# One product of 512 columns instead of two of 256 in the query, gate and output projections of the first block

## The chip, the cores and the metric
The kernel runs on one core of a Trainium2 chip. The metric is the device time of one execution in microseconds (us), the median of several runs. A profile of one execution comes beside it. Engines: PE (TensorE) multiplies, PEld is its weight load, DVE (VectorE), ACT (ScalarE) and POOL (GpSimd) do the rest, and SP issues most DMAs.

## The reference
Two transformer blocks run over 256 tokens in float32. Only the first block's mixer matters here (16 learned tokens are put in front, so 272):

```
u = rms_norm(h, mix_pre_g);  proj = u @ w_in
hq, hf, hi, hg, cq, ckv, kpe, gates = split(proj)
y_a = hgrn2_mixer(hq, hf, hi, hg, ...) @ w_hg_o     # qh = silu(hq): a scan over the tokens
y_b = mla_mixer(cq, ckv, kpe, ...)     @ w_mla_o    # attention with latent q, k, v
gate_a, gate_b = split(sigmoid(gates + b_gate))
mixed = (gate_a * y_a + gate_b * y_b) @ w_out
h = h + rms_norm(mixed, mix_post_g)                 # then the feed-forward part, then block 2
```

## The kernel before, in words
Each float32 matrix is used as a high part (rounded to what a fast product takes) and a low part (the rest). A product is high weights by high tokens, high weights by low tokens, and low weights by high tokens, added in PSUM.

**Weights.** They come in slabs of 16 blocks of 128 x 128 (SP's queue, three buffers `raw`), and a slab is two *units* of eight blocks. A step `split u` makes the parts of unit u: `wh` by ACT or DVE (a copy with rounding), `wl` by POOL or DVE (a subtraction). The letters in `MADE` (L412) say who does which; they are not changed. A unit can be split when its place in `WH` and `WL` was read by PE.

**Tokens.** `OPERAND[src][:, k, part, :]` holds token rows k, both parts side by side: x1 is the normed input (272 columns a part), oh the scan's output, om the attention's (256 a part).

**Tiles.** `gemm name n` computes 128 output columns of a projection for all tokens: eight row blocks (k), three products of 256 columns each (`three`, L861) into the first 256 columns of a PSUM bank. `evac name n` takes the result from PSUM. Names: `hq` (query of the scan, 8 tiles), `gate` (16 tiles, 0 to 7 for y_a, 8 to 15 for y_b), `ya` and `yb` (the two output projections, 8 each), `kn`, `qn`, `qpe`, `ckv`, `cq`, `kpe`, `hf`, `hg` and others, which stay as they are. The feed-forward tiles g1, u1, g2, u2 are already `FOLDED` (L842, L961): one product of 512 columns (high weights by both parts) and one of 256 (low weights), after which the two halves of the bank are added.

**Order.** One list `ORDER` of steps is written by `segments` and woven by the strings in `MIX`. Each engine walks that list and issues its own instructions of each step, so every engine has a fixed order; semaphores tie them. The stages here, with the time of the trace: hq tiles (69 to 92 us), then the scan (to 185) with its steps `level` (PE), `decay` (DVE, multiplies queries and keys), `k_turn`, `state`, `read` and the latent norms `lat` between tiles hg, ckv, kpe, cq and gate 0 to 7; then kn, qn, qpe (to 211); gate 8 to 15 and ya between the attention's heads (`m_score`, `m_exp`, `m_turn`, `m_value`, to 282); yb (to 305); `down out1` 0 to 3 and the first `tail` (w_out, whose weights are units 76 to 83).

**Before the change.** In `scalar` and `vector`: hq n is a sigmoid on ACT from PSUM and a multiplication on DVE with PSUM (L1317, L1646). gate n is one tanh on ACT from PSUM (L1326). ya n is one DVE product with PSUM (L1667). yb n is a DVE product with PSUM, a DVE addition of ya's part, an ACT copy that makes the high part of `mx` and a DVE product minus that for the low part (L1340, L1672); `mx` is what `down out1` multiplies. gate and ya use PSUM banks 0, 1, 2 in turn, yb 0 to 3, hq all eight; a bank is free when the last reader of a tile is done.

Of the kernel before, what the change touches and what calls it, by code (L numbers as in the profile page):

```python
# [556 lines left out]
def rf(ap):  # L557
    return ap.bitcast(FP)


def program(nc, dr):
    ctx = ExitStack()
    with ctx:
# [278 lines left out]
        FOLDED = ("g1", "u1", "g2", "u2")  # L842
# [11 lines left out]
        def tensor(e):  # L854
# [43 lines left out]
            for step in ORDER:  # L898
# [52 lines left out]
                elif kind == "gemm":  # L951
# [4 lines left out]
                    for k in range(k0, k1):  # L956
                        u, o = divmod(BLOCK_AT[step] + k - k0, 8)
                        unit(u, o)
                        e.wait_ge(*act.at(part(src, "h", k)))
                        e.wait_ge(*dve.at(part(src, "l", k)))  # L960
                        if name in FOLDED:  # L961
                            e.matmul(b.rearrange("p (a t) -> p a t", a=2), whi(u, o), OPERAND[src][:, k, :, :], start=k == 0, stop=False)
                            m = e.matmul(b[:, 0:256], wlo(u, o), operand(src, k, 0), start=False, stop=k == 7)
                        else:
                            m = three(b[:, 0:t.stop - t.start], whi(u, o), wlo(u, o), operand(src, k, 0)[:, t],
                                      operand(src, k, 1)[:, t], k == 0, k == kt - 1)
                        names = ([("used", u)] if o == 7 else []) + ([use] if k == kt - 1 else [])
                        if names:
                            m.then_inc(*pe.up(*names))
# [296 lines left out]
        def scalar(e):  # L1266
            e.dma_start(cst[:, 0:128], dr["cst"][:, 0:128]).then_inc(*in_id.up("all", by=16))
            e.wait_ge(*dve.at("one"))
            e.activation(stat("one"), stat("one"), ACT.Sqrt)
            for step in ORDER:  # L1270
# [37 lines left out]
                elif kind == "evac":  # L1308
# [8 lines left out]
                    elif name in ("hq", "hg"):  # L1317
# [8 lines left out]
                    elif name == "gate":  # L1326
                        e.wait_ge(*pe.at(use))
                        e.wait_ge(*dve.at("half_bias"))
                        if n >= 8:
                            e.wait_ge(*pe.at(("read", 1, 1)))  # L1330
                        e.activation((GA0 if n < 8 else GA1)[:, n % 8, :], b[:, 0:256], ACT.Tanh, bias=sc("b_gate", n),
                                     scale=0.5).then_inc(*act.up(step))
                        banks.ended(use, act.now())
                    elif name in ("kn", "qn"):
                        e.wait_ge(*pe.at(use))
# [227 lines left out]
        def vector(e):  # L1563
            e.memset(rf(R2[:, 0:512]), 1.0).then_inc(*dve.up("unread"))
            for name in ("one", ("one", "out1"), ("one", "ffn1"), ("one", "out2"), ("one", "ffn2")):
                e.memset(stat(name), 1.0).then_inc(*dve.up(name))
            for step in ORDER:
# [62 lines left out]
                elif kind == "evac":  # L1630
# [15 lines left out]
                    elif name in ("hq", "hg"):  # L1646
                        v = (Qr if name == "hq" else SG)[:, n, :]
# [19 lines left out]
                    elif name == "ya":  # L1667
                        e.wait_ge(*act.at(("evac", "gate", n)))
                        e.wait_ge(*pe.at(use))
                        e.scalar_tensor_tensor(GA0[:, n, :], GA0[:, n, :], 1.0, b[:, 0:256], ALU.add, ALU.mult).then_inc(*dve.up(step))  # L1670
                        banks.ended(use, dve.now())
                    elif name == "yb":  # L1672
                        g = GA1[:, n, :]
                        e.wait_ge(*act.at(("evac", "gate", 8 + n)))
                        e.wait_ge(*pe.at(use))
                        e.scalar_tensor_tensor(g, g, 1.0, b[:, 0:256], ALU.add, ALU.mult).then_inc(*dve.up(step))
                        banks.ended(use, dve.now())
# [641 lines left out]
```

## Time and profile before

| | us |
|---|---|
| median of 3 runs (lowest, highest) | 927.81 (926.04, 928.13) |
| profiled execution, its own time | 925.93 |
| its span, first to last instruction | 924.1 |
| PE busy in the span | 902.4 |
| DVE, ACT, POOL busy | 678.8, 465.2, 223.1 |

The span is what the engines' rows cover; the rest of the execution's time lies around it. The granted TensorE clock was 0.997 of full speed. Matmul rows overlap, so the pace of PE is read from start to start. In a timeline a row is a start, a duration, the engine, the line, the operation, what it writes and reads by the program's names, and how many instructions it merges; a bracket gives the engine's idle time before it and who ended it. All helpers record at one line per kind, so groups are told apart by names and shapes: `pb` is PSUM, `R` the token operands, `wh` and `wl` the weight parts, `FA` the working area, `st` small statistics.

### The profile page before, as it was taken

The numbers are of one execution on the slowest core, as the hardware profiler recorded it, in microseconds if no ns is written. First come the engines' busy times: TensorE is split into PE (matmuls) and PEld (weight loads), VectorE is DVE, ScalarE is ACT, GpSimd is POOL, SyncE is SP. The second block draws the span as 40 slices with busy tenths as digits, with TensorE's granted clock in tenths as the row PEclk, the third lists the DMA queues.
The fourth block names the chain that finished last, engine by engine and source line by source line (L and its number), as shares of the span: only waits on it lengthen the run. The fifth ranks groups of instructions, "written<-read, shape, count | busy, mean of one in ns | idle before, by whom it ended". The sixth has DMA issues, their size and how long they took to land.

```text
span 924.1 us, 16815 instructions
## 1 busy us (share of the span) xinstructions
PE 902.4 (98%) x6767; PEld 800.5 (87%) x6767; DVE 678.8 (73%) x1274; ACT 465.2 (50%) x936; POOL 223.1 (24%) x120
## 2 busy tenths in 40 slices
PE   9999999999999999999999999999999999999996
PEld 8879999889999888888888799887988888888885
DVE  5924986658655888767576768868888888788885
ACT  6334336564443574434444647776634445544343
POOL 3433421441213211642314342231100211210121
PEclk9999999999999999999999999999999999999999
DMA  8454444233433645655545354324445555455521
GB/s 296 150 205 143 176 141 139 84 122 138 137 105 130 227 175 207 226 184 194 197 162 222 136 191 157 106 87 163 179 157 208 183 188 209 155 223 183 214 105 46
DMA packets 23181, 153.67 MB, mean 166 GB/s; under 512 B 2864, under 2 KB 3248, under 8 KB 5568
## 3 DMA queue, kind: packets, MB, share of 16 engines
q1 hardware_dynamic: 22384, 150.43, 45.6%
q0 software_dynamic: 576, 2.10, 0.6%
q8 instruction: 54, 0.88, 0.4%
q14 instruction: 23, 0.19, 0.1%
q10 hardware_dynamic: 144, 0.07, 0.0%
HBM read 151.28 MB, written 1.05 MB: 165 GB/s over the span
## 4 chain that ended last, share of the span: by engine, by line
PE 60%; DVE 26%; ACT 10%; issue 4%; DVEq 0%; ACTq 0%
PE pb L506 58%; DVE wl L515 11%; ACT wh L512 4%; DVE FA L515 4%; DVE FA L518 4%; DVE FA L521 3%; ACT FA L512 3%; PE pb L509 2%; DVE wh L530 1%; ACT R L512 1%; DVE X L521 1%; DVE R L521 1%; DVE st L518 0%; DVE post L518 0%; DVE FA L524 0%
## 5 line engine op out<-in xcount | busy, mean ns | idle before, releaser
L506 PE MATMUL pb<-R,wh 128*128 128x256 f32 (+2 forms) x2224 | 550.4, 326 | 5.9 <-ACT R L512 2.0
L506 PE MATMUL pb<-R,wl 128*128 128x256 f32 (+1 forms) x1512 | 422.7, 281 | 0.0
L506 PEld LDWEIGHTS pb<-R,wh 128*128 128x128 f32 x2224 | 372.2, 189 | 45.4 <-ACT R L512 3.5
L515 POOL TENSOR_TENSOR wl<-raw,wh 128x1024 fp32r<-128x1024 f32 (+1 forms) x80 | 195.7, 2450 | 632.8 <-ACT wh L512 522.7
L515 DVE TENSOR_TENSOR wl<-raw,wh 128x1024 fp32r<-128x1024 f32 (+1 forms) x198 | 262.0, 1345 | 82.1 <-ACT wh L512 80.5
L506 PEld LDWEIGHTS pb<-R,wl 128*128 128x128 f32 x1512 | 284.3, 188 | 2.0 <-issue 0.3
L512 ACT ACTIVATE wh<-raw 128x1024 fp32r<-128x1024 f32 (+1 forms) x219 | 222.8, 1044 | 52.8 <-PE pb L506 50.8
L506 PE MATMUL pb<-wh,R 128*128 128x512 f32 (+2 forms) x724 | 234.4, 388 | 4.1 <-DVE R L515 2.1
L506 PEld LDWEIGHTS pb<-wh,R 128*128 128x128 f32 (+1 forms) x724 | 134.4, 186 | 36.7 <-ACT R L512 4.0
L512 ACT ACTIVATE FA<-pb 128x256 f32<-128x256 f32 (+7 forms) x240 | 94.0, 414 | 125.9 <-PE pb L506 111.0
L506 PE MATMUL pb<-wl,R 128*128 128x512 f32 (+2 forms) x372 | 143.3, 385 | 0.0
L512 ACT ACTIVATE FA<-FA 128x256 f32<-128x256 f32 (+4 forms) x69 | 28.0, 405 | 141.3 <-DVE FA L521 121.8
L506 PEld LDWEIGHTS pb<-wl,R 128*128 128x128 f32 (+1 forms) x372 | 68.2, 183 | 12.7 <-issue 0.2
L515 DVE TENSOR_TENSOR FA<-pb,FA 128x256 f32<-128x256 f32 (+1 forms) x128 | 53.9, 426 | 34.3 <-ACT FA L512 34.3
L515 DVE TENSOR_TENSOR FA<-FA 128x256 f32<-128x256 f32 (+7 forms) x120 | 68.9, 598 | 8.5 <-ACT FA L512 3.3
L506 PE MATMUL pb<-FA 128*32 128x16 f32 (+6 forms) x1456 | 60.9, 216 | 0.2
L512 ACT ACTIVATE R<-FA 128x256 fp32r<-128x256 f32 (+1 forms) x66 | 28.4, 431 | 61.7 <-DVE FA L515 61.7
L506 PEld LDWEIGHTS pb<-FA 128*32 128x32 f32 (+3 forms) x1456 | 53.0, 132 | 7.0 <-issue 1.5
L530 DVE CAST wh<-raw 128x1024 fp32r<-128x1024 f32 (+1 forms) x59 | 45.1, 765 | 11.9 <-PE pb L506 11.9
L515 DVE TENSOR_TENSOR R<-FA,R 128x256 fp32r<-128x256 f32 (+1 forms) x58 | 26.9, 464 | 28.9 <-ACT R L512 28.9
L512 ACT ACTIVATE FA<-FA,st 128x256 f32<-128x256 f32 (+2 forms) x65 | 29.3, 453 | 9.8 <-DVE st L518 9.6
L521 DVE SCALAR_TENSOR_TENSOR FA<-FA,sm 128x255 f32<-128x255 f32 x64 | 30.9, 483 | 2.3
(122 smaller groups left out, 474.4 us busy)
## 6 DMA issues: line engine op xcount, KB each, us to landing
raw<-in_w SPq DMA_DIRECT2D x137, 1024.0 KB, 4.8
X<-in_x SPq DMA_DIRECT2D x2, 512.0 KB, 4.3
raw<-in_w SPq DMA_DIRECT2D x2, 512.0 KB, 6.5
post<-in_ffn_post SPq DMA_DIRECT2D x2, 512.0 KB, 4.6
post<-in_w POOLq DMA_DIRECT2D x2, 512.0 KB, 5.0
FA<-in_w POOLq DMA_DIRECT2D x2, 512.0 KB, 7.9
out<-X SPq DMA_DIRECT2D x4, 256.0 KB, 2.0
cst<-in_cst SPq DMA_DIRECT2D x1, 821.5 KB, 12.4
```

The source lines that it names most:

```text
L506: return self.real.matmul(*a, **k) if self.real else self
L509: return self.real.transpose(*a, **k) if self.real else self
L512: return self.real.activation(*a, **k) if self.real else self
L515: return self.real.tensor_tensor(*a, **k) if self.real else self
L518: return self.real.tensor_scalar(*a, **k) if self.real else self
L521: return self.real.scalar_tensor_tensor(*a, **k) if self.real else self
L530: return self.real.tensor_copy(*a, **k) if self.real else self
```

## The change
hq, gate, ya and yb become folded. Their first product takes both token parts (512 columns), so a tile uses a whole PSUM bank. ACT copies the second half of the bank to an area in SBUF (`other`), DVE adds the first half to it; after this the bank is free. hq's and gate's functions then run from SBUF, and for hq and gate one tile later in ACT's order (`query(n - 1)` and `gated(n - 1)` stand in tile n's place; the last ones in the place of hg 0, kn 0 and ya 0). hq's multiplication on DVE is likewise one tile later. The unit order, who splits what, and the list of steps are the same. The gate tiles had no DVE instruction; now they have one.

```diff
-        FOLDED = ("g1", "u1", "g2", "u2")
+        FOLDED = ("g1", "u1", "g2", "u2", "hq", "gate", "ya", "yb")
+        def other(name, n):
+            return {"hq": Tt[1][:, 256 * (n % 4):256 * (n % 4) + 256], "gate": (GA0 if n < 8 else GA1)[:, n % 8, :],
+                    "ya": rope2[n % 2][:, 0:256], "yb": rope2[n % 2][:, 0:256]}[name]
...
-                            e.matmul(b.rearrange("p (a t) -> p a t", a=2), whi(u, o), OPERAND[src][:, k, :, :], start=k == 0, stop=False)
-                            m = e.matmul(b[:, 0:256], wlo(u, o), operand(src, k, 0), start=False, stop=k == 7)
+                            e.matmul(b.rearrange("p (a t) -> p a t", a=2), whi(u, o), OPERAND[src][:, k, :, t], start=k == 0, stop=False)
+                            m = e.matmul(b[:, 0:256], wlo(u, o), operand(src, k, 0)[:, t], start=False, stop=k == 7)
...
         def scalar(e):
+            def query(n):
+                e.wait_ge(*dve.at(("folded", "hq", n)))
+                e.wait_ge(*dve.at(("evac", "hq", n - 4)))
+                e.wait_ge(*dve.at(("evac", "hf", 7)))
+                e.activation(other("hq", n), Qr[:, n, :], ACT.Sigmoid).then_inc(*act.up(("evac", "hq", n)))
+            def gated(n):
+                g = other("gate", n)
+                e.wait_ge(*dve.at(("folded", "gate", n)))
+                e.activation(g, g, ACT.Tanh, bias=sc("b_gate", n), scale=0.5).then_inc(*act.up(("evac", "gate", n)))
...
+                    elif name == "hq":
+                        if n:
+                            query(n - 1)
                         e.wait_ge(*pe.at(use))
                         e.wait_ge(*pool.at("lev"))
-                        e.activation((Qr if name == "hq" else SG)[:, n, :], b[:, 0:256], ACT.Sigmoid).then_inc(*act.up(step))
+                        e.activation(Qr[:, n, :], b[:, 256:512], ACT.Copy).then_inc(*act.up(("side", *use[1:])))
+                        banks.ended(use, act.now())
...
-                        e.activation((GA0 if n < 8 else GA1)[:, n % 8, :], b[:, 0:256], ACT.Tanh, bias=sc("b_gate", n),
-                                     scale=0.5).then_inc(*act.up(step))
+                        g = other(name, n)
+                        e.activation(g, b[:, 256:512], ACT.Copy).then_inc(*act.up(("side", *use[1:])))
                         banks.ended(use, act.now())
+                        if n % 8:
+                            gated(n - 1)
...
+                    elif name == "ya":
+                        if n == 0:
+                            gated(15)
+                        e.wait_ge(*pe.at(use))
+                        e.wait_ge(*dve.at(("evac", "qpe", 3)))
+                        e.wait_ge(*dve.at(("evac", "ya", n - 2)))
+                        e.activation(other(name, n), b[:, 256:512], ACT.Copy).then_inc(*act.up(("side", *use[1:])))
+                        banks.ended(use, act.now())
                     elif name == "yb":
+                        e.wait_ge(*pe.at(use))
+                        e.wait_ge(*dve.at(("evac", "ya", n + 6)))
+                        e.wait_ge(*dve.at(("evac", "yb", n - 2)))
+                        e.activation(other(name, n), b[:, 256:512], ACT.Copy).then_inc(*act.up(("side", *use[1:])))
+                        banks.ended(use, act.now())
                         e.wait_ge(*dve.at(("mix", n)))
...
         def vector(e):
+                    elif name == "gate":
+                        g = other(name, n)
+                        e.wait_ge(*act.at(("side", *use[1:])))
+                        e.tensor_tensor(g, b[:, 0:256], g, ALU.add).then_inc(*dve.up(("folded", *use[1:])))
+                        banks.ended(use, dve.now())
...
-                        e.scalar_tensor_tensor(g, g, 1.0, b[:, 0:256], ALU.add, ALU.mult).then_inc(*dve.up(step))
-                        banks.ended(use, dve.now())
+                    elif name == "yb":
+                        g, y = GA1[:, n, :], other(name, n)
+                        e.wait_ge(*act.at(("side", *use[1:])))
+                        e.tensor_tensor(y, b[:, 0:256], y, ALU.add).then_inc(*dve.up())
+                        banks.ended(use, dve.now())
+                        e.wait_ge(*dve.now())
+                        e.wait_ge(*act.at(("evac", "gate", 8 + n)))
+                        e.scalar_tensor_tensor(g, g, 1.0, y, ALU.add, ALU.mult).then_inc(*dve.up(step))
```

DVE's hq and ya follow the same pattern (the hq multiplication stands in the next tile's place; ya's product takes `y` instead of PSUM).

On ACT, around the first square root of the latent norms (`LN<-LN`) and gate 3; `FA<-pb,sm` is a tanh from PSUM, `FA<-FA,sm` one from SBUF:

```order
 L512 ACTIVATE FA<-pb 64x8x64 x2
 L512 ACT_TABLE_LOAD
 L512 ACTIVATE LN<-LN 128x272
-L512 ACT_TABLE_LOAD
-L512 ACTIVATE FA<-pb,sm 128x256
+L512 ACTIVATE FA<-pb 128x256
+L512 ACT_TABLE_LOAD
+L512 ACTIVATE FA<-FA,sm 128x256
 L512 ACTIVATE FA<-pb 128x512
 L512 ACTIVATE R<-post 128x272 x2
 L512 ACTIVATE FA<-pb 128x512
```

Gate 3's copy stands ahead of the table load, and the tanh after it is gate 2's.

On DVE at the same place (`LN<-pb` is the latent norm's variance, then split 44):

```order
 L530 COPY FA<-pb 128x512
 L518 TENSOR_SCALAR LN<-pb 128x272
+L515 TENSOR_TENSOR FA<-pb,FA 128x256
 L530 CAST wh<-raw 128x1024
 L515 TENSOR_TENSOR wl<-raw,wh 128x1024
```

Gate 3's add stands between the variance and the split.

On DVE in yb, two tiles, the first without a split of DVE's behind it:

```order
-L521 SCALAR_TENSOR_TENSOR FA<-FA,pb 128x256
+L515 TENSOR_TENSOR FA<-pb,FA 128x256
+L521 SCALAR_TENSOR_TENSOR FA<-FA 128x256
 L515 TENSOR_TENSOR FA<-FA 128x256
 L521 SCALAR_TENSOR_TENSOR R<-FA,R 128x256
-L521 SCALAR_TENSOR_TENSOR FA<-FA,pb 128x256
+L515 TENSOR_TENSOR FA<-pb,FA 128x256
+L521 SCALAR_TENSOR_TENSOR FA<-FA 128x256
 L515 TENSOR_TENSOR FA<-FA 128x256
 L521 SCALAR_TENSOR_TENSOR R<-FA,R 128x256
 L515 TENSOR_TENSOR wl<-raw,wh 128x1024
```

The product no longer reads PSUM, and the add stands in front of it.

## Rows read from the trace of the kernel before

**Rows 1.** The page: its parts 1 and 4, PE's busy time and the chain.
```profile
PE 902.4 (98%) x6767; PEld 800.5 (87%) x6767; DVE 678.8 (73%) x1274; ACT 465.2 (50%) x936; POOL 223.1 (24%) x120
...
PE 60%; DVE 26%; ACT 10%; issue 4%; DVEq 0%; ACTq 0%
```
**Rows 2.** Timeline of PE, first products of hq 0 and hq 2.
```profile
69.33 0.40 PE L506 MATMUL pb<-R,wh 128*128 128x256 f32 x2
...
75.03 0.40 PE L506 MATMUL pb<-R,wh 128*128 128x256 f32 x2
```
**Rows 3.** Timeline of PE, a g1 tile's first product, and what follows the u1 tile.
```profile
380.71 0.40 PE L506 MATMUL pb<-R,wh 128*128 128x512 f32 x1
...
386.30 0.39 PE L506 MATMUL pb<-wh,R 128*128 128x512 f32 x1
```
**Rows 4.** Timeline of PE, first products of yb 1 and yb 3.
```profile
285.09 0.40 PE L506 MATMUL pb<-R,wh 128*128 128x256 f32 x2
...
290.85 0.40 PE L506 MATMUL pb<-R,wh 128*128 128x256 f32 x2
```
**Rows 5.** Groups by line and shape, ACT and DVE: busy us, mean ns, idle before.
```profile
L512 ACT ACTIVATE FA<-pb 128x256 f32<-128x256 f32 x144 | 49.8, 373 | 78.8 <-PE pb L506 78.8
...
L515 DVE TENSOR_TENSOR FA<-pb,FA 128x256 f32<-128x256 f32 x124 | 51.2, 418 | 22.8 <-ACT FA L512 22.8
```
**Rows 6.** Timeline of ACT, hq 7's sigmoid.
```profile
92.35 0.38 ACT L512 ACTIVATE FA<-pb 128x256 f32<-128x256 f32 x1 [2.47 <-PE pb L506]
```
**Rows 7.** Timeline of ACT in the scan: split 43, square root, latent squares.
```profile
154.82 1.05 ACT L512 ACTIVATE wh<-raw 128x1024 fp32r<-128x1024 f32 x1
...
160.67 0.43 ACT L512 ACTIVATE LN<-LN 128x272 f32<-128x272 f32 x1 [2.54 <-DVE LN L518]
...
166.42 0.72 ACT L512 ACTIVATE LN<-CQ 128x256 f32<-128x256 f32 x2
```
**Rows 8.** Timeline of DVE in the scan: six decays, then split 44.
```profile
157.05 2.64 DVE L515 TENSOR_TENSOR FA<-FA 128x512 f32<-128x512 f32 x6
...
160.56 0.68 DVE L530 CAST wh<-raw 128x1024 fp32r<-128x1024 f32 x1
```
**Rows 9.** Timeline of PE in the scan: k_turn's transposes, second latent sum.
```profile
159.84 0.63 PE L509 MATMUL pb<-cst,FA 128*128 128x128 f32 x4 [0.79 <-DVE FA L515]
...
167.33 1.06 PE L506 MATMUL pb<-LN,cst 128*128 128x256 f32 x4
```
**Rows 10.** Timeline of ACT: table load before gate 8, first exponential.
```profile
216.55 1.28 ACT L512 ACT_TABLE_LOAD   x1
...
220.47 0.41 ACT L512 ACTIVATE FA<-FA,st 128x144 f32<-128x144 f32 x1
```
**Rows 11.** Timeline of all engines near 224 us.
```profile
223.45 0.29 DVE L524 CUSTOM_DVE_ANT_0 FA<-pb,cst 128x144 f32<-128x144 f32 x1
...
224.11 0.71 PE L509 MATMUL pb<-cst,FA 128*128 128x128 f32 x5
```
**Rows 12.** Timeline of DVE in yb: tiles 1 to 3, and split 79.
```profile
288.75 0.41 DVE L521 SCALAR_TENSOR_TENSOR FA<-FA,pb 128x256 f32<-128x256 f32 x1
...
291.06 1.23 DVE L515 TENSOR_TENSOR wl<-raw,wh 128x1024 fp32r<-128x1024 f32 x1 [0.52 <-ACT wh L512]
292.20 0.42 DVE L521 SCALAR_TENSOR_TENSOR FA<-FA,pb 128x256 f32<-128x256 f32 x1
...
295.30 2.06 DVE L521 SCALAR_TENSOR_TENSOR R<-FA,R 128x256 fp32r<-128x256 f32 x1 [0.49 <-ACT R L512]
...
310.34 1.23 DVE L515 TENSOR_TENSOR wl<-raw,wh 128x1024 fp32r<-128x1024 f32 x1 [0.52 <-ACT wh L512]
```
**Rows 13.** Timeline of POOL, split 74.
```profile
294.56 2.52 POOL L515 TENSOR_TENSOR wl<-raw,wh 128x1024 fp32r<-128x1024 f32 x1 [10.85 <-ACT wh L512]
```
**Rows 14.** Timeline of DVE and of PE: split 83, and the product behind it.
```profile
317.15 1.23 DVE L515 TENSOR_TENSOR wl<-raw,wh 128x1024 fp32r<-128x1024 f32 x1
...
318.53 0.47 PE L506 MATMUL pb<-wh,R 128*128 128x512 f32 x1 [0.17 <-DVE wl L515]
```

More of the change, by code:

```diff
@@ L1330, in scalar @@
                             e.wait_ge(*pe.at(("read", 1, 1)))
[L1331 to L1332 removed]
+                        g = other(name, n)
+                        e.activation(g, b[:, 256:512], ACT.Copy).then_inc(*act.up(("side", *use[1:])))
                         banks.ended(use, act.now())
+                        if n % 8:
+                            gated(n - 1)
                     elif name in ("kn", "qn"):
+                        if use[1:] == ("kn", 0):
+                            gated(7)
                         e.wait_ge(*pe.at(use))
@@ L1563, in vector, with query @@
         def vector(e):
+            def query(n):
+                e.wait_ge(*act.at(("evac", "hq", n)))
+                e.tensor_tensor(Qr[:, n, :], Qr[:, n, :], other("hq", n), ALU.mult).then_inc(*dve.up(("evac", "hq", n)))
             e.memset(rf(R2[:, 0:512]), 1.0).then_inc(*dve.up("unread"))
@@ L1645, in vector @@
                         e.tensor_scalar(Km[:, n, :], Fm[:, n, :], -1.0, 1.0, ALU.mult, ALU.add).then_inc(*dve.up(step))
-                    elif name in ("hq", "hg"):
-                        v = (Qr if name == "hq" else SG)[:, n, :]
+                    elif name == "hq":
+                        v = Qr[:, n, :]
+                        e.wait_ge(*act.at(("side", *use[1:])))
+                        e.tensor_tensor(v, b[:, 0:256], v, ALU.add).then_inc(*dve.up(("folded", *use[1:])))
+                        banks.ended(use, dve.now())
+                        if n:
+                            query(n - 1)
+                    elif name == "gate":
[3 more added lines that the diff above has]
+                        banks.ended(use, dve.now())
+                    elif name == "hg":
+                        if n == 0:
+                            query(7)
+                        v = SG[:, n, :]
                         e.wait_ge(*act.at(step))
@@ L1667, in vector @@
                     elif name == "ya":
-                        e.wait_ge(*act.at(("evac", "gate", n)))
-                        e.wait_ge(*pe.at(use))
-                        e.scalar_tensor_tensor(GA0[:, n, :], GA0[:, n, :], 1.0, b[:, 0:256], ALU.add, ALU.mult).then_inc(*dve.up(step))
+                        y = other(name, n)
+                        e.wait_ge(*act.at(("side", *use[1:])))
+                        e.tensor_tensor(y, b[:, 0:256], y, ALU.add).then_inc(*dve.up())
+                        banks.ended(use, dve.now())
+                        e.wait_ge(*dve.now())
+                        e.wait_ge(*act.at(("evac", "gate", n)))
+                        e.scalar_tensor_tensor(GA0[:, n, :], GA0[:, n, :], 1.0, y, ALU.add, ALU.mult).then_inc(*dve.up(step))
+                    elif name == "yb":
+                        g, y = GA1[:, n, :], other(name, n)
+                        e.wait_ge(*act.at(("side", *use[1:])))
+                        e.tensor_tensor(y, b[:, 0:256], y, ALU.add).then_inc(*dve.up())
                         banks.ended(use, dve.now())
-                    elif name == "yb":
-                        g = GA1[:, n, :]
+                        e.wait_ge(*dve.now())
                         e.wait_ge(*act.at(("evac", "gate", 8 + n)))
-                        e.wait_ge(*pe.at(use))
-                        e.scalar_tensor_tensor(g, g, 1.0, b[:, 0:256], ALU.add, ALU.mult).then_inc(*dve.up(step))
-                        banks.ended(use, dve.now())
+                        e.scalar_tensor_tensor(g, g, 1.0, y, ALU.add, ALU.mult).then_inc(*dve.up(step))
                         e.wait_ge(*dve.now())
```

7 lines of the change are left out of this document (6 added, 1 removed).

## Prediction, written before the result was known
> **What bounds the kernel now.** I read the page first, then the list of who waited for whom on PE, then the timelines of PE, ACT, DVE and POOL through the first block (0 to 330 us), where every edit lies. The page says that PE is busy in 98% of the span [rows 1], and that the chain that ended last is 60% PE, but 26% DVE and 10% ACT [rows 1]. Between 40 and 318 us PE has no long wait. That doesn't mean that there is room: each engine works in its written order, and several products start less than a microsecond after the DVE or ACT result that they need. So there are two questions: what a product of 512 columns saves on PE, and how much of the added ACT and DVE work arrives too late for a PE product that has little to spare.
>
> Below, times are those of the trace of before, and "+x" at such a time means that the changed kernel reaches that point x later.
>
> **What PE gains.** A block of eight weight rows was three products of 256 columns per row (24 in a tile); now it is one of 512 and one of 256 (16 in a tile). 320 products and as many weight loads go, but the columns stay 768 per row. Two hq tiles, 16 rows of weights, took 75.03 - 69.33 = 5.70 us [rows 2]; two tiles of g1/u1, already in the new form, 386.30 - 380.71 = 5.59 us [rows 3]. That is 0.055 us per tile. Two yb tiles took 5.76 us [rows 4], so 0.085 each there. 24 tiles of hq and gate at 0.055, 8 of ya at about 0.045 and 8 of yb at 0.085 make 1.3 + 0.4 + 0.7 = 2.4 us, 0.26% of the span. From below, the new form could gain nothing at the source x1, whose two parts lie 272 apart, not 256 (then 1.1 us); more than 2.4 is excluded by rows 3, which is the same form. The Trainium skill (TensorE: Matmul & The Clock Gate, Back-to-back issue gap) gives N/2.4 + 2.5 ns for one product's gap, which would make the merge worth 2.5 ns a row, 0.8 us in all; the rows show 7 ns a row, and I use them.
>
> **What ACT and DVE pay.** Each of the 40 tiles now has an ACT copy of PSUM columns 256 to 511 (0.37 us [rows 5]) and a DVE add of the first half (0.42 us [rows 5]): 15 us of ACT and 17 us of DVE. Most of it lies in idle time. What matters is where it stands in the order.
>
> *hq (69 to 95 us), hidden.* The last tile's chain becomes copy, add, sigmoid, multiply, and an ACT split of 1.05 us and a DVE one of 1.22 us stand inside it. The tile ends at 92.35 [rows 6] less 0.45, the gain of eight tiles; copy to 92.3, add to 92.8, ACT split to 93.25, sigmoid to 93.6, DVE split to 94.5, multiply to 94.9. The second diag product, at 95.66 before, needs it at 95.2: 0.3 us to spare. The gain of 0.45 is kept so far.
>
> *gate 0 to 3, the gain is lost.* DVE had no gate work before; now its add waits for the copy. In the stretch from 143 to 157 us ACT is the chain: gate 1's and gate 2's places take a copy and a tanh instead of a tanh, +0.37 each, so the ACT split at 154.82 [rows 7] starts when it did before, though PE is 0.6 ahead. DVE's split and its six decays, from 157.05 [rows 8], follow it and end at 159.69; the transpose on PE that waited 0.79 us for them [rows 9] starts at 159.86 instead of 159.84. The lead of hq and four gate tiles is gone.
>
> *gate 3 to 5, PE falls behind.* In ACT's order gate 3 stands behind the square root at 160.67 [rows 7] and in front of a table load of 1.28 us (a load of that kind is in rows 10). Before, DVE went straight on at 160.56 with its split [rows 8]. Now its order is: add of gate 3 first, and that waits for a copy which can only run after the root (161.15 to 161.53). Add to 162.0, cast and split to 163.86 (+1.36), reciprocal to 165.6, two products to 166.6. ACT's copies to R at 164.84 start at 166.2 (+1.36), then k_turn's copy, gate 4's copy and tanh (+0.37), and the two squares at 166.42 start at 168.1 and end at 168.8. The product on PE at 167.33 started 0.19 us behind those squares; it now starts at about 169.0 [rows 7, 9]: **+1.65**. Queued behind it on PE are state 1 and all reads. State 0 on DVE is +2.2 for the same reason, but PE, then 1.7 later itself, needs it 0.9 us after its old end, so it adds nothing.
>
> *gate 8 and 9.* The table load at 216.55 ran while gate 8 waited [rows 10]. Now it stands behind gate 9's copy, which waits for PE until 218.5: load to 220.2, tanh, split, and the exponentials at 220.47 start at 221.55, +1.07. DVE's reduce at 223.45 (after a reciprocal and two scalings) is +1.07 with them; it frees what the transposes at 224.11 need [rows 11], with 0.34 to spare: +0.73 beyond what PE already has. From there to yb the tiles only save: 0.11 for gates 6 and 7, 0.3 for gates 10 to 15, 0.35 for ya. The ya tiles add 0.8 to 1.3 us to DVE's lateness, but the products that wait there had 1.0 to 2.7 us. At yb 0 (282.14) PE stands at 1.65 - 0.11 + 0.73 - 0.3 - 0.35 = **+1.6**.
>
> *yb, the largest term.* Here DVE and ACT already run a ring per tile: DVE product with PSUM, DVE add, ACT copy to R, ACT split, DVE split; 292.20 - 288.75 = 3.45 us [rows 12] against PE's 2.88. The change puts the fold's add in front of it, 0.46 us more start to start, so 3.91. The side copy hides behind DVE's split, except after the two tiles whose split goes to POOL: there DVE used to go on at once, and now waits for a copy that stands behind ACT's split, 0.9 us. And the product with PSUM becomes one with both inputs in SBUF. What that can cost is in [rows 12, 13]: the product R<-FA,R at 295.30 took 2.06 us instead of 0.42 and ended 0.28 us after POOL's split (294.56 to 297.08); it is so again at 304.92. The Trainium skill (SBUF — State Buffer, Who interferes with whom) says that a DVE instruction with two SBUF inputs contends with a GpSimd one that reads SBUF, and the later one blocks until the other ends. Rows 12 and 13 agree, and by the rule the new product is open to it at all 16 ya and yb tiles; without it the term is 4.3, below.
> Tile by tile, with POOL's split moved along, DVE's split in tile's place ends at 289.6 (72), 293.5 (73), then 302.0 (75, blocked by POOL once), 305.9 (76), 314.3 (78, blocked once more), 318.3 (79): before, the last ended at 311.57 [rows 12], so **+6.8**. PE meets this as it comes: it is 0.7 ahead from its own tiles, then down 1 needs POOL's split of unit 77, which ends at 311.0 and not 306.7 (+2.9), down 2 unit 78 (+3.5), down 3 unit 79 (+4.9), and the row of weights at 318.53 unit 83. There PE already waited for DVE [rows 14]; DVE's split of 83, ended 318.38, now ends at 324.7, as units 81 and 82 stand in front of it and the idle 0.4 and 0.7 us there are used up. So **+6.3** from 282.14 to 318.53, the 0.7 saved included. If the new product is never blocked, DVE is two times 1.0 us less late: +4.3. POOL and SP keep their order. SP's load for units 84 and 85 waits for units 78 and 79 and lands 4.8 us after, 323.2, when DVE, at 324.7, has not come to it yet. Nothing after 318.53 is touched, and all of it hangs on the same engines, late by the same amount, so nothing is given back.
>
> **Sum.** +1.6 at yb 0, +6.3 in yb and down: +7.9 us. The profiled execution took 925.93 us (span 924.1 and 1.8 around it); with 7.9 it is 933.8. The median of the runs shown is 927.81, so the forecast is **935.7 us**, +0.85%. Lower bound of the costs: no blocking (-2.0), gate 8 and 9 absorbed (-0.7), half of the wait at 167.33 absorbed (-0.8): +4.4, 932.2. Upper: two or three more DVE instructions blocked for 1 us each: +10.5, 938.3.
>
> **The rivals.**
> *1. The chains are late, but nothing is blocked and slack absorbs the scan.* For it: POOL works only 24% of the time, and the fold's product misses it if DVE is a microsecond later than I make it. Against: POOL's split is let go by the same ACT split as the work in question. +2.5 to +4.3: about 931.2 us.
> *2. Faster.* One mechanism: the DVE add never holds DVE. If ACT's copy is always done by the time DVE gets there and the ring in yb (3.45 us before) is shortened by what DVE waits for ACT (0.48 and 0.52 us a tile in rows 12), then PE keeps its tiles' gain, and the time is 927.8 - 2.4 = 925.4. It decides at yb: DVE's lateness at unit 79 must stay under the 1.9 us which PE had to spare (the split ended at 311.57, the product that needs it started at 313.4). Against: these waits are in the ring's own path, the added 0.46 us is not beside them, and the copy behind the square root at 161 is not early by any reading of rows 7.
> *3. It comes out even.* Costs of 2 to 3 us, as one of the two places (167.33 or yb) absorbs, against 2.4 gained: 928.0.
> *4. The new product is slower at x1,* whose parts lie 272 columns apart: no row shows a 512 product with this step. A product of 256 takes 5.70 / 48 = 0.119 us; if a row of weights took half of one more, 192 rows would cost 11.4 us beside the waits: 947. Against: the products of rows 3 run at full rate, with parts 256 apart.
> *5. Longer waits:* each place costs as forecast, and ya blocks too (8 products open to POOL's splits at 255 to 280): +10 to +14, 940.
>
> **How the numbers follow.** The forecast as it stands (932.5 to 938.5) has 0.60; rival 1 0.14, rival 2 0.06, rival 3 0.07, rival 4 0.03, rival 5 0.10. 0.2% is 1.9 us, about what a measurement of this kernel tells from no change. Faster: rival 2, 0.06. Same: rival 3, and a little of rival 1, 0.07. Slower: the rest, 0.87. The range for 8 in 10 takes in the forecast's case and most of rival 1, and ends short of rivals 4 and 5: 930.8 to 938.8.
>
> **What the profile after would show.** Right: 16 products per tile at 2.79 us in hq and yb; the first wait of PE at the transpose near 159.9 grown from 0.8 to about 1.4 us; a new wait of PE for ACT of about 1.7 us at the product that stood at 167.33; one of 0.8 near 225; DVE's split every 3.9 us in yb, DVE products FA<-FA of 2 us there next to POOL's, and waits of PE for splits of 1 to 3 us each through down and the first tail. Wrong, if PE shows no wait between 160 and 320 us, or if the g1 stage starts less than 4 us later than before.

## The result, and the profile after

The changed kernel takes 935.6 us (median of 4 executions, 934.63 to 936.26) against 927.47 us: ratio 1.0090, 95% interval 1.0077 to 1.0103. It is slower by 0.9%; 935.7 was forecast. The profiled executions are 935.1 (span 933.3) and 925.93 (span 924.1), 9.2 us apart. Parts 1 and 4 of the page after, against [rows 1]:

```profile
PE 900.8 (97%) x6447; PEld 781.8 (84%) x6447; DVE 696.8 (75%) x1314; ACT 477.2 (51%) x976; POOL 222.6 (24%) x120
...
PE 78%; DVE 13%; ACT 7%; issue 2%; DMA 0%; DVEq 0%; SPq 0%; ACTq 0%
```

320 products are gone, but PE's busy time fell by only 1.6 us, while DVE's grew by 18 and ACT's by 12 us (17 and 15 were forecast). The time went into waits of PE, and the list of who waited for whom on PE gives them:

```profile
PE pb L506 <- DVE wl L515: 4.9, 7, 1.2
...
PE pb L509 <- ACT FA L512: 2.9, 3, 1.5
PE pb L506 <- DVE R L515: 2.3, 1, 2.3
PE pb L506 <- POOL wl L515: 2.1, 1, 2.1
...
PE pb L506 <- DVE wh L530: 1.4, 1, 1.4
...
PE pb L506 <- issue: 0.8, 1, 0.8
```

(Total us, times, longest.) Before, the first line was 1.6 us in three waits, the `issue` line 0.2 us, and the POOL and the `DVE wh` line were not there. `issue` is time in which PE waited for nothing that the profile shows; below I call it a halt. In the timeline of PE these are the new or longer waits up to 328 us; an idle time ahead of a row is in its brackets:

```profile
101.61 0.49 PE L506 MATMUL pb<-FA 128*32 128x16 f32 x35 [0.76 <-issue]
...
147.93 1.15 PE L506 MATMUL pb<-FA 128*64 128x64 f32 x32 [0.74 <-DVE FA L515]
149.24 1.15 PE L506 MATMUL pb<-FA 128*64 128x64 f32 x32 [0.15 <-DVE FA L515]
160.77 0.63 PE L509 MATMUL pb<-cst,FA 128*128 128x128 f32 x4 [0.58 <-DVE FA L515]
169.71 0.45 PE L506 MATMUL pb<-LN,cst 128*128 128x256 f32 x1 [1.39 <-DVE wh L530]
227.19 0.74 PE L509 MATMUL pb<-cst,FA 128*128 128x128 f32 x5 [0.74 <-DVE st L524]
308.94 0.47 PE L506 MATMUL pb<-wh,R 128*128 128x512 f32 x1 [0.85 <-DVE wl L515]
...
314.02 0.47 PE L506 MATMUL pb<-wh,R 128*128 128x512 f32 x1 [2.08 <-POOL wl L515]
...
317.42 0.47 PE L506 MATMUL pb<-wh,R 128*128 128x512 f32 x1 [0.40 <-DVE wl L515]
...
321.34 0.47 PE L506 MATMUL pb<-wh,R 128*128 128x512 f32 x1 [0.93 <-DVE wl L515]
...
327.68 0.48 PE L506 MATMUL pb<-wh,R 128*128 128x512 f32 x1 [0.93 <-DVE wl L515]
```

The wait at 169.71 is put down to DVE's cast, which ends 0.09 us ahead of it. ACT's squares end at 169.57, 0.14 us ahead, and in the run e11 below PE starts this product 0.17 us behind the squares, before that cast has ended. So it isn't the cast; what is left is ACT's squares, as forecast.

Setting each step of PE beside the same step of before gives how late PE is at each point:

| PE's step | start before, us | later by, us | forecast, us |
|---|---|---|---|
| diag 0 | 95.10 | -0.4 | -0.45 |
| product of hg 2 behind level (0,0) | 101.88 | +0.15 | -0.45 |
| level (1,5) | 148.06 | +1.2 | about -0.6 |
| k_turn 0 | 159.84 | +0.9 | 0.0 |
| latent sum, `lat cq 1` | 167.33 | +2.4 | +1.65 |
| m_turn 0 | 224.11 | +3.1 | +2.3 |
| yb 0 | 282.14 | +2.8 | +1.6 |
| down 1 | 308.00 | +6.0 | |
| down 3 | 313.44 | +7.9 | |
| tail (0,1) | 319.30 | +9.2 | +7.9 |

So yb and down took 6.3 us as forecast (9.15 - 2.81), and the part ahead of yb took 2.8 where 1.6 was forecast. DVE's timeline in yb shows both effects of the forecast, against [rows 12, 13]:

```profile
292.35 0.42 DVE L515 TENSOR_TENSOR FA<-pb,FA 128x256 f32<-128x256 f32 x1
...
296.26 0.41 DVE L515 TENSOR_TENSOR FA<-pb,FA 128x256 f32<-128x256 f32 x1
...
299.30 0.42 DVE L515 TENSOR_TENSOR FA<-pb,FA 128x256 f32<-128x256 f32 x1 [0.79 <-ACT FA L512]
299.75 2.01 DVE L521 SCALAR_TENSOR_TENSOR FA<-FA 128x256 f32<-128x256 f32 x1
...
311.75 0.42 DVE L515 TENSOR_TENSOR FA<-pb,FA 128x256 f32<-128x256 f32 x1 [0.79 <-ACT FA L512]
312.21 1.95 DVE L521 SCALAR_TENSOR_TENSOR FA<-FA 128x256 f32<-128x256 f32 x1
```

and POOL's, in the same stretch:

```profile
299.07 2.41 POOL L515 TENSOR_TENSOR wl<-raw,wh 128x1024 fp32r<-128x1024 f32 x1 [12.27 <-ACT wh L512]
311.53 2.35 POOL L515 TENSOR_TENSOR wl<-raw,wh 128x1024 fp32r<-128x1024 f32 x1 [10.04 <-ACT wh L512]
```

The ring is 296.26 - 292.35 = 3.91 us a tile. At each tile whose split goes to POOL, DVE waits 0.79 us for the next side copy, and its product with both inputs in SBUF ends 0.28 us behind POOL's split, as 2.01 us instead of 0.42.

**A thing to know for all comparisons below.** Executions of one kernel lie up to 3.5 us apart. Most of that goes with the granted clock: of 67 executions of the kernel before, the 11 whose mean clock was 0.999 have a median of 925.9 us, the 31 at 0.995 of 927.9. In 12 of the 14 profiles, though in neither of the two above, it falls near the end, during or after PE's wait of 2.1 to 2.4 us for DVE at 909 to 919; the run e3 below shows what that is:

```profile
911.12 0.47 PE L506 MATMUL pb<-wh,R 128*128 128x512 f32 x1 [2.35 <-DVE R L515]
...
911.74 1.05 PE L506 MATMUL pb<-wh,R 128*128 128x512 f32 x2
...
915.29 0.63 PE L506 MATMUL pb<-wh,R 128*128 128x512 f32 x2
```

Two products take 1.05 us instead of 0.63 for 3.4 us: the clock is at 1.2 GHz instead of 2.4, and PE loses 1.6 us (1.5 to 1.6 in each of the twelve). The clock also falls for 3.4 us at 331 to 333 in e3, e10 and e11, where PE loses 0.7 to 0.9 us and keeps that loss, at 314 in e6, and at 646 to 649 in the kernel before, e1, e2, e3 and e12, where about 1.1 us are lost and are back by 651. So a median can't tell less than about 1 us here, and where the cause is at issue I read how late PE is in the trace ahead of such a fall.

### The profile page after: what moved, and what is told of

Same layout as the page of the kernel before. It is cut to its first block, busy times and chain, and to the rows that moved or that the text cites. A ratio compares the mean times of both kernels' runs of the same rounds, so it can differ in the third digit from the quotient of the medians.

```text
span 933.3 us, 16261 instructions
## 1 busy us (share of the span) xinstructions
PE 900.8 (97%) x6447; PEld 781.8 (84%) x6447; DVE 696.8 (75%) x1314; ACT 477.2 (51%) x976; POOL 222.6 (24%) x120
## 3 DMA queue, kind: packets, MB, share of 16 engines
HBM read 151.28 MB, written 1.05 MB: 163 GB/s over the span
## 4 chain that ended last, share of the span: by engine, by line
PE 78%; DVE 13%; ACT 7%; issue 2%; DMA 0%; DVEq 0%; SPq 0%; ACTq 0%
PE pb L506 76%; DVE wl L515 3%; DVE FA L515 3%; ACT FA L512 3%; ACT wh L512 2%; DVE FA L518 2%; PE pb L509 2%; ACT R L512 1%; DVE FA L521 1%; DVE X L521 1%; DVE R L521 0%; DVE wh L530 0%; DVE FA L524 0%; DMA X<-in_x 0%; DVE st L518 0%
## 5 line engine op out<-in xcount | busy, mean ns | idle before, releaser
L506 PE MATMUL pb<-R,wh 128*128 128x512 f32 (+2 forms) x1904 | 547.0, 352 | 6.0 <-ACT R L512 2.0
L506 PEld LDWEIGHTS pb<-R,wh 128*128 128x128 f32 x1904 | 332.4, 188 | 58.6 <-ACT R L512 3.5
L512 ACT ACTIVATE FA<-pb 128x256 f32<-128x256 f32 (+7 forms) x272 | 105.8, 409 | 138.1 <-PE pb L506 127.7
L515 DVE TENSOR_TENSOR FA<-pb,FA 128x256 f32<-128x256 f32 (+1 forms) x160 | 67.4, 425 | 49.8 <-ACT FA L512 49.6
L512 ACT ACTIVATE FA<-FA 128x256 f32<-128x256 f32 (+4 forms) x77 | 31.3, 406 | 142.7 <-DVE FA L521 121.8
L515 DVE TENSOR_TENSOR FA<-FA 128x256 f32<-128x256 f32 (+4 forms) x128 | 73.7, 598 | 8.5 <-ACT FA L512 3.3
L509 PE MATMUL pb<-cst,FA 128*128 128x128 f32 (+3 forms) x196 | 28.0, 275 | 5.4 <-ACT FA L512 2.9
```

Of the source, the lines that this page charges most:

```text
L506: return self.real.matmul(*a, **k) if self.real else self
L509: return self.real.transpose(*a, **k) if self.real else self
L512: return self.real.activation(*a, **k) if self.real else self
L515: return self.real.tensor_tensor(*a, **k) if self.real else self
```

## Experiments

All were made from one source: the changed kernel with a list of tiles that keep three products, their old ACT and DVE steps and their old place in the order.

```diff
+        def folds(name, n):
+            return name in FOLDED and (name, n) not in APART
...
-                        if name in FOLDED:
+                        if folds(name, n):
```

By its construction, with every tile in that list its instructions are those of the kernel before, with none, those of the changed one.

**One group of tiles at a time.** The list holds all but hq (e1), gate 0 to 7 (e2), gate 8 to 15 and ya (e3), yb (e4).

> Only the eight hq tiles have the new form; gate, ya and yb are as before. Theory (the loss is made at four places, none of them in hq): PE keeps the 0.4 us of these tiles, and the trace of the changed kernel showed one wait of PE's own issue of 0.76 us in level (0,0) at 100.9 where before one of 0.24 us stood at 96.7, so -0.4 to +0.2 us, 927.3 against 927.5. Rival (every new tile costs its added ACT and DVE work, 8.1 us over 40 tiles, 0.2 us each): +1.6 us, 929.1.

> Only gate 0 to 7 in the new form. Theory: gate 0's add in front of the decays of level 4 on DVE moves them behind the start of POOL's split at 145 us, one of them takes over 3 us instead of 1.2, and PE waits about 0.7 to 1.0 us for it at level (0,5); gate 3's copy behind the square root makes PE wait 1.4 us at the latent sum near 169. Sum +2.2 us, 929.7. Rival (0.2 us a tile): +1.6 us without these two waits, and DVE's decays of level 4 at their old 1.4 us.

> Only gate 8 to 15 and ya in the new form. Theory: one wait of 0.7 us at the transposes near 224 (gate 9's copy in front of the table load), less 0.7 us which 16 tiles save on PE: 0 to +0.4 us, 927.7. Rival (0.2 us a tile): +3.2 us, 930.7.

> Only the eight yb tiles in the new form. Theory: DVE's ring grows from 3.45 to 3.91 us a tile, waits 0.8 us for the side copy after each of POOL's two splits (units 74, 77), its product with both inputs in SBUF is held by them to 2 us, and PE waits for the splits of units 77, 79 and 83: +6.4 us, 933.9. Rival (0.2 us a tile): +1.6 us, 929.1. If the ring's length alone counted, without POOL: about 4.3 us, 931.8.

| new form only in | us | ratio to before (95%) | PE later in the trace |
|---|---|---|---|
| hq (e1) | 928.4 | 1.0014 (1.0005 to 1.0023) | -0.7 at 102, +1.5 from 144 on |
| gate 0 to 7 (e2) | 929.9 | 1.0031 (1.0021 to 1.0041) | +0.9 at 148, +0.6 at 160, +2.1 at 167 |
| gate 8 to 15, ya (e3) | 928.2 | 1.0013 (1.0003 to 1.0023) | +0.8 at 224, +0.5 at 282 |
| yb (e4) | 934.2 | 1.0080 (1.0067 to 1.0092) | +3.3 at down 1, +6.4 at the tail |

The rival of an even 0.2 us a tile falls: eight yb tiles cost 6.9 us, sixteen of gate and ya 1.0. e2 and e4 came as expected, e3 0.6 us above it by the median and as expected in the trace up to 282 us (its profile then loses 0.9 us in the fall of the clock at 331), all three with PE's waits where they were named: e4 alone has the 2.08 us wait for POOL at down 1 and 6.4 us at the tail. e1 missed: +1.2 us instead of at most 0.2. Its trace shows one loss, and it is none of the terms of the forecast:

```profile
141.53 0.39 PE L506 MATMUL pb<-R,wh 128*128 128x256 f32 x2
141.76 0.28 PE L506 MATMUL pb<-R,wl 128*128 128x256 f32 x1
141.89 0.40 PE L506 MATMUL pb<-R,wh 128*128 128x256 f32 x2
144.30 0.28 PE L506 MATMUL pb<-R,wl 128*128 128x256 f32 x1 [2.02 <-issue]
```

PE stands still for 2.02 us in the middle of gate 0, a tile which e1 leaves as it was, with all its data there.

**What the halts of PE hang on.** I counted PE's records (products, weight loads, waits on semaphores) in front of each such halt. In the kernel before, e2, e3, e4, e10, e11 and e12 the halt is at 96.8 to 97.2 us, in hg 1; in the changed kernel, e5, e6, e7 and e8 at 100.9 to 101.7, in level (0,0); always at record 1473, behind the 718th product. In e1 that record falls in level (0,0) too, and there is a small stop: 0.32 us from one product to the next, where its neighbours take 0.01. In e1, e5 and e8 there is a halt at 143.6 to 144.3 us, always at record 3265. These are 1792 apart, seven times 256; none of these kernels has one at the six places between them, each 256 on. e9 puts that to the test: new form in hq 0 to 3 alone. (In it the sigmoid of hq 3 and its multiplication are left out.)

> Only hq 0 to 3 in the new form: 32 products and 32 weight loads fewer ahead of the scan, half of what the run with all hq tiles left out. Theory (PE halts at fixed counts of its own records, 1473 and 3265 so far, seven times 256 apart, whatever stands there): the halt is again at record 1473, which now lies in hg 2 near 100.6, or at record 3265, which now lies in the products of level (1,4) near 141.3, and nowhere else; sizes 0.2 to 2 us, so the time is 927.5 to 928.5 (0.2 us of tiles saved). Rival (the halts follow the products at 97, 101 or 144 themselves): a halt at one of these old places.

It took 926.9 us, ratio 0.9992 (0.9983 to 1.0002). The list of waits has no halt this time, but record 1473 is where it was expected, in hg 2, and a small stop is to be seen there: the product behind a `wl` row starts 0.12 us after it everywhere else in this tile, here 0.43.

```profile
99.33 0.40 PE L506 MATMUL pb<-R,wh 128*128 128x256 f32 x2
99.56 0.28 PE L506 MATMUL pb<-R,wl 128*128 128x256 f32 x1
99.99 0.39 PE L506 MATMUL pb<-R,wh 128*128 128x256 f32 x2
```

At record 3265 (140.95, in the products of level (1,4)) there is none. A second stop, which the theory hadn't named, comes behind record 1729, exactly 256 on, inside a level whose 64 products take 1.05 us here and 0.74 before:

```profile
102.71 1.05 PE L506 MATMUL pb<-FA 128*32 128x16 f32 x64
```

So the place of the first follows the count, which the theory said, and the new one lies on the same count in steps of 256; the size (up to 0.8 us at 1473; 0, 0.43, 0.50 and 2.02 at 3265) differs from execution to execution and from place to place, and it was read from one execution of each kernel. It comes in or after runs of 64 or 128 short products (128 in 1.3 us), which use up records more than ten times as fast as the tiles do. The Trainium skill (Runtime: NRT & Kernel Launch, Instruction fetch mechanics) says that an engine's instructions are fetched in blocks of 256, mostly hidden. The distances of 1792 and 256 agree with that; if the halts are this fetch, the 2.02 us shows that it isn't always hidden. That it is the fetch of code I take from the count and that page; no run here showed the fetch itself.

**Gate 0 and gate 3.** Three runs: the changed kernel with gate 0 apart (e5); only gate 1 to 7 (e10); only gate 0 to 7 without 3 (e11).

> The changed kernel, but gate 0 keeps its three products and its tanh from PSUM, so DVE has no add in front of the decays of level 4. Theory (decays pushed under POOL's split at 145 us): the three decays take 1.4 us again instead of 3.6, PE's wait of 0.74 us at level (0,5) goes, and the later points move with it: -0.7 to -1.0 us against the changed kernel, ratio to before 1.008 instead of 1.009. Rival (PE's later waits, at the transposes near 160 and the sum near 169, swallow it): no change, 1.009. A wait of PE's own issue may come up elsewhere, as it did near 143 when only hq was in the new form; that would hide the gain and is read from the trace.

> Gate 1 to 7 in the new form, gate 0 and all else as before (no hq, so PE's records up to 142 us are those of the kernel before). Theory: without gate 0's add the decays of level 4 take 1.4 us again and PE's wait of 0.73 us at level (0,5) goes; the ACT chain of 143 to 157 us is then later by gate 1's and gate 2's extra 0.3 us alone, the wait at the transposes near 160 by 0.2 us; gate 3 still costs 1.2 to 1.4 us at the sum near 168. -0.5 us against the run with gate 0 to 7, 929.3. Rival (gate 0's add costs nothing beyond what gates 1 and 2 cost on ACT): 929.9.

> Gate 0, 1, 2 and 4 to 7 in the new form, gate 3 and all else as before. Theory (gate 3's copy behind the square root holds DVE's split and reciprocal): PE's wait of 1.4 us at the latent sum near 169 falls to 0.2 to 0.4 us (gate 4's copy is left in ACT's order ahead of the squares), what stays is the 0.6 us of gates 0 to 2: -1.1 us against the run with gate 0 to 7, 928.8. Rival (gate 4's copy and tanh ahead of the squares make the wait): 929.7.

Measured: e5 937.4 us, 1.0103 (1.0086 to 1.0120); e10 927.6, 1.0009 (0.9999 to 1.0019); e11 928.8, 1.0010 (1.0001 to 1.0019). e5 missed: 1.8 us above the changed kernel, where 0.7 to 1.0 below it had been expected. PE's wait at level (0,5) was gone, but two halts at records 1473 and 3265 had put PE 0.7 us later by then, which left the same lateness at k_turn, and at 328 us both traces are 9.2 us late. What makes e5 longer comes later, 1.6 us of it in the fall of the clock at 920, which the profile after lacks. Between 144.7 us, behind both halts, and k_turn PE falls behind by 0.2 us in e5 and by 0.9 in the changed kernel, so as far as it goes this trace agrees with e10. e10 and e11 start from the records of the kernel before and are clean. What was wrong at gate 0 is in DVE's timeline after, with gate 0's add in front of six decays:

```profile
143.96 0.42 DVE L515 TENSOR_TENSOR FA<-pb,FA 128x256 f32<-128x256 f32 x1 [1.26 <-ACT FA L512]
144.30 4.88 DVE L515 TENSOR_TENSOR FA<-FA 128x512 f32<-128x512 f32 x6
```

and POOL after:

```profile
144.95 2.87 POOL L515 TENSOR_TENSOR wl<-raw,wh 128x1024 fp32r<-128x1024 f32 x1 [16.26 <-ACT wh L512]
```

In e10, where the add isn't there, the decays start as they did before and take 2.70 us, ahead of POOL's split:

```profile
142.10 2.70 DVE L515 TENSOR_TENSOR FA<-FA 128x512 f32<-128x512 f32 x6
```

The add waits for a copy, that pushes the decays from 142.10 to 144.30, there one of them meets POOL's split and is held, and level (0,5) gets its data 0.7 us late. It is the blocking of the yb stage at a place where I had not looked for it. e10's PE is on time at level (0,5) and 0.2 us late at k_turn, against 0.8 in e2 (each measured from where the two stood at 98 us); the price of gate 0 is 0.6 us.

Not all of that is the blocking. e10 also takes out gate 0's tanh, which in the changed kernel stands in gate 1's place on ACT. k_turn hangs on that chain: ACT, then DVE's decays. ACT before, and after:

```profile
147.56 1.05 ACT L512 ACTIVATE wh<-raw 128x1024 fp32r<-128x1024 f32 x1
148.50 1.72 ACT L512 ACTIVATE FA<-FA 32x256 f32<-32x256 f32 x4
```

```profile
147.51 0.50 ACT L512 ACTIVATE FA<-FA,sm 128x256 f32<-128x256 f32 x1
147.91 1.05 ACT L512 ACTIVATE wh<-raw 128x1024 fp32r<-128x1024 f32 x1
149.13 1.73 ACT L512 ACTIVATE FA<-FA 32x256 f32<-32x256 f32 x4 [0.17 <-PE pb L506]
```

The tanh takes 0.40 us of ACT's time, start to start, and the forecast had it. Behind the split ACT then goes on after 1.22 us instead of 0.94, as it waits for PE's level (0,5): 0.3 us, and that alone is what the blocking costs at k_turn. e2, e6, e7 and e11 show the same 0.17 us of idle time; e5 and e10, without gate 0's add, show none, nor does e8, whose second halt falls just ahead. e10's median is 2.3 us below e2's, more than the 0.5 expected; at 167 us its trace is only 0.6 earlier, and the rest I don't put down to gate 0.

e11 settles gate 3. ACT's timeline of the changed kernel, then that of e11:

```profile
161.60 0.43 ACT L512 ACTIVATE LN<-LN 128x272 f32<-128x272 f32 x1 [2.54 <-DVE LN L518]
161.94 0.37 ACT L512 ACTIVATE FA<-pb 128x256 f32<-128x256 f32 x1
...
166.96 0.85 ACT L512 ACTIVATE R<-post 128x272 fp32r<-128x272 f32 x2 [2.34 <-DVE post L521]
```

```profile
161.70 0.43 ACT L512 ACTIVATE LN<-LN 128x272 f32<-128x272 f32 x1 [2.54 <-DVE LN L518]
...
165.86 0.84 ACT L512 ACTIVATE R<-post 128x272 fp32r<-128x272 f32 x2 [1.06 <-DVE post L521]
```

Without gate 3's copy and add the wait for DVE's work falls from 2.34 to 1.06 us, and PE's latent sum starts with no wait at all (168.25, 0.9 late, which it was from gate 0 on): 1.5 us for one tile. 1.1 of it is the copy and the add, by which ACT's copies to R start later (166.96 against 165.86). The other 0.4 is gate 3's tanh: in the changed kernel it stands in gate 4's place, ahead of the squares, and e11 takes it out too. The rival, gate 4's place on ACT, is thus worth 0.4 us; the forecast had it in its sum.

**What in yb costs.** Three edits of the changed kernel: the sum of ya and yb is left in PSUM (e6); POOL makes 8 of 1024 columns of units 74 and 77 (e7); the side copy and add of yb 4 to 7 stand one tile earlier, the add in DVE's wait for the copy to R (e8).

```diff
-                        e.tensor_tensor(y, b[:, 0:256], y, ALU.add)
+                        e.tensor_tensor(b[:, 0:256], b[:, 0:256], y, ALU.add)      # e6
...
+                    if u in (74, 77):
+                        c = slice(0, 8)                                            # e7
...
                         e.tensor_tensor(g, g, GA0[:, n, :], ALU.add).then_inc(*dve.up(("mix", n)))
+                        if n + 1 in AHEAD:
+                            summed(n + 1)                                          # e8
```

> The changed kernel, but ya and yb leave the sum of the two parts in PSUM and the product reads it there, so the product has one input in SBUF. Theory (an instruction with both inputs in SBUF waits until POOL's split ends): the product at 299.75 takes 0.4 us, but the addition behind it, whose inputs both lie in SBUF, is held instead and ends with POOL's split; the gain is 0.3 to 0.5 us at each of two places, under 1 us in all. Rival (it is the product's own form that is slow beside POOL): 1.6 us each, 3.2 us in all.

> The changed kernel, but POOL's splits of units 74 and 77 make only 8 of their 1024 columns, so the low weights of these units are left out for the most part. This takes POOL's 2.4 us out of yb and keeps all waits. Theory: both products of 2.0 us fall to 0.42 (3.1 us off DVE's chain), PE's wait for unit 77 goes, what stays is the ring of 3.91 us a tile and the two waits for the side copy: about -3.0 us against the changed kernel, 932.6. Rival (POOL's splits are beside the chain): no change, 935.6.

> The changed kernel, but the side copy of yb 4 to 7 stands before ACT's copy to R of the tile ahead, and DVE adds its parts in the gap of 0.48 us in which it waits for that copy. Theory (the ring's length is the loss): DVE's splits of units 76 to 79 come 3.5 us a tile apart instead of 3.91, the wait of 0.8 us for the side copy at tile 6 goes, unit 79 is ready 2.0 to 2.6 us earlier and unit 83 with it: -2.3 us, 933.3. Rival (ACT then becomes the late one): 0 to -1 us.

Measured: e6 935.5 us, 1.0086 (1.0071 to 1.0101); e7 933.0, 1.0060 (1.0045 to 1.0075); e8 933.5, 1.0066 (1.0051 to 1.0081); 932.6 and 933.3 had been expected of the last two. In e6 the wait only moved one instruction on, from the product to the addition behind it:

```profile
299.27 0.42 DVE L521 SCALAR_TENSOR_TENSOR FA<-FA,pb 128x256 f32<-128x256 f32 x1
299.73 1.53 DVE L515 TENSOR_TENSOR FA<-FA 128x256 f32<-128x256 f32 x1
```

So it is not the product's form that is slow. From yb 0 to the tail PE loses 5.4 us in this trace instead of 6.3, so the gain of up to 1 us is there, and the median can't show it. In e7, with POOL's split at 0.21 us, the product at the same place takes its normal time:

```profile
299.03 0.42 DVE L521 SCALAR_TENSOR_TENSOR FA<-FA 128x256 f32<-128x256 f32 x1
```

and PE is 3.8 us earlier than in the changed kernel at down 2 (0.7 of that it had at 102 us already), of which 3.6 are left at 675 us. In e8 the adds at 302.16, 305.62 and 309.08 lie in the old waits of 0.48 us, tiles come 3.46 us apart instead of 3.91, and PE is 3.2 us earlier at the tail:

```profile
302.16 0.42 DVE L515 TENSOR_TENSOR FA<-pb,FA 128x256 f32<-128x256 f32 x1
...
305.62 0.42 DVE L515 TENSOR_TENSOR FA<-pb,FA 128x256 f32<-128x256 f32 x1
```

Both parts of the term, the length of the ring and POOL's hold on it, are shown. e7 and e8 together weren't run.

But what e7 takes out is not what the change added, for the kernel before had two such holds as well [rows 12]. In the tile with the first of them DVE's rows before, then the same stretch after, are:

```profile
293.93 0.42 DVE L521 SCALAR_TENSOR_TENSOR FA<-FA,pb 128x256 f32<-128x256 f32 x1
...
297.28 1.21 DVE L515 TENSOR_TENSOR wl<-raw,wh 128x1024 fp32r<-128x1024 f32 x1
```

```profile
303.66 1.23 DVE L515 TENSOR_TENSOR wl<-raw,wh 128x1024 fp32r<-128x1024 f32 x1 [0.53 <-ACT wh L512]
```

From the product to DVE's next split it is 2.3 us in a tile without a hold (288.75 to 291.06 in [rows 12]), 3.35 us before with one, and 303.66 - 299.75 = 3.91 after. So a hold cost 1.0 us before and costs 1.6 now. DVE falls behind by 6.5 us from yb 0 to the split of unit 79: 3.7 are the eight adds, 1.7 the two waits for the side copy (0.85 each), and only 1.1 are the two holds.

**Where it pays.** New form in gate 10 to 15 and ya only.

> The new form only where PE's later products have room behind it: gate 10 to 15 and ya, 14 tiles; hq, gate 0 to 9 and yb as before. Theory: no wait is added; the tiles save 0.02 to 0.05 us each, which the run with gate 8 to 15 and ya showed as 0.35 us from 224 to 282 us: -0.3 to -0.5 us, 927.0 against 927.4, within what can be told from no change. Rival (DVE's later work in ya comes out at yb): +0.5 us.

926.9 us against 927.6, ratio 0.9993 (0.9985 to 1.0002). PE shows no added wait and is 0.3 us early at 255 us. That is what these 14 tiles save, and it can't be told from no change. No version beats the kernel before by more than the measurement tells.

## Why the prediction was right, and where it was not

The sign, the size and the main mechanism were right; that the sum came to 935.7 so exactly is luck.

*Right.* The new form saves 0.05 us per hq tile (0.4 in eight) and 0.1 per yb tile (2.77 us instead of 2.88 from yb 1 on; [rows 4]). Gate 3 behind the square root: forecast +1.65 at the latent sum, measured 1.4 to 1.5 (e2, e11). Gate 9 ahead of the table load: forecast +0.73, PE's wait is 0.74. yb: ring 3.91 forecast and measured; two products blocked, two measured; 6.3 forecast, 6.3 measured. Rival 1 (nothing blocked) falls with the trace after, where two products are held; its price for that case, 2.0 us less, was too small, as e7 puts the two holds at 3.1. Rival 2 (faster) falls with e4, rival 3 (even) with the result. Rival 4, a slower 512 product at x1, falls too: the first hq tile starts a row of weights every 0.35 us, 2.8 us a tile. Rival 5 had ya blocked too, and PE shows no wait there.

*Wrong.* The part ahead of yb, by 1.2 us: 0.9 too little at k_turn (points 1 and 2), 0.2 too much at the latent sum, 0.1 too little at m_turn, 0.4 too little behind it (point 3). Two of the signs named for being right missed as well: PE's wait at the transpose near 159.9 is 0.58 us and not 1.4, and those for the splits are 0.4 to 2.1 us and not 1 to 3.

1. "The transpose on PE that waited 0.79 us for them starts at 159.86 instead of 159.84." It started at 160.77. I had followed ACT's chain from 143 us on and left out what gate 0's add does to DVE's decays, the blocking by POOL at 145 us. I counted what a move costs in instructions and not what the moved ones meet where they land. Of the 0.6 us between e2 and e10 it is 0.3; the rest is gate 0's tanh, which was in the sum.
2. "The gain of 0.45 is kept so far." It was lost at level (0,0), to a halt of PE's own (0.76 us instead of 0.24). The edit shortened PE's stream by 128 records, and that moved the halt into the run of short products. No term of the sum had that, and the lead that was to pay for gate 1's and gate 2's places on ACT was gone: from 0.4 early at 95 us to 0.15 late at 102, 0.5 us, the larger part of the 0.9 at k_turn. Gate 1's copy on ACT starts at 147.23, as before (147.19), and not 0.6 earlier.
3. "0.3 for gates 10 to 15, 0.35 for ya": together 0.3 came (m_turn 0 to yb 0). ya's gain per tile, put at 0.045, is nothing: from 255 to 282 us a row of weights starts every 0.35 us, before (2.82 us a tile) and after (2.82). No row of the forecast was from ya; a gate tile saves 0.04.

*Compensated.* The traces differ by 9.2 us, the medians by 8.1. My correction from the profiled execution to the median, 1.9 us, belongs to the kernel before, whose profiled execution was one of its shorter ones; the changed kernel's own correction is 0.5 us. So the sum of 7.9 was 1.3 too small against its own measure, and the clock gave about that back: at a mean clock of 0.999 the two executions of the changed kernel (934.63, 935.1) have a mean 8.9 us above the median of 925.9 of the kernel before.

## What to carry to other kernels

Fewer and wider products save almost nothing when the columns stay the same: 0 to 0.1 us a tile here, and what pays is set by what the extra copy and add stand in front of on ACT and DVE. One tile's added steps at the wrong place cost 1.5 us, fourteen tiles elsewhere cost nothing. Before a hold is counted as a cost of a change, look whether the kernel before pays for it too: here 2.1 of 3.1 us were there already. When an instruction is put in front of others, follow those to their new time and look at what POOL runs there: in these traces a DVE instruction with both inputs in SBUF that starts beside a split of POOL's waits for it. And an edit to the number of PE's instructions moves its halts for the whole program, so a change of a few tenths of a per cent has to be read from a trace step by step, not from a median.

## What was not expected of the hardware

- PE halts at fixed counts of its own records, 1473 and 3265 (seven times 256 apart), for 0.2 to 2.02 us, with all data ready, in or behind runs of 64 to 128 products of 16 to 32 columns. All fourteen kernels show the first in the place where that record fell, twelve of them in the list of waits, e1 and e9 as a stop of 0.3 us; only e1, e5 and e8 show the second, and e9 alone one at 1729, 256 behind the first.
- The same wait of 2.1 to 2.4 us near the end was followed by the lower clock in 12 of 14 profiles and not in the other two; it costs 1.5 to 1.6 us. Executions with a mean clock of 0.999 are 2.0 us shorter than those at 0.995.
- When an instruction is held by POOL, moving one of its inputs to PSUM doesn't help if the one behind it has both in SBUF: it is held instead (1.53 us, e6).
